# A hybrid decoder step on one core: the front in chunks of 256, 384 and 392 tokens, without index queries for the first

## The chip, the cores and the metric

The kernel is one program on one core of a Trainium2 chip. Its time is device microseconds of one execution, from start to end; less is better. The profile is of one execution of its own, in which the span is the time from the first instruction to the last.

## The reference, cut to what matters

One layer of a hybrid decoder: 1024 prompt tokens (positions 0 to 1023), and 8 sample sequences of one token each behind 1024 cached ones. One input projection feeds sparse attention (group A) and a gated linear recurrence (group B).

```python
h = einsum('btd,de->bte', rms_norm(x, ln_g), w_in)       # D = 1024, columns of 11 parts
# A) lightning indexer, one score for each visible key
s = einsum('bthd,bsd->bths', iq, ik) * IDX_DIM ** -0.5    # 8 index heads of 64
score = einsum('bths,bth->bts', relu(s), iw)
score = where(causal, score, -inf)
_, idx = lax.top_k(score, 256)                            # TOPK_MAX 256, for prompt and sample
out = sparse_attn(q, k[idx], v[idx], ...)                 # 8 heads, 4 kv heads, bias by distance
# B) HGRN2: f = lb + (1 - lb) * sigmoid(h_f); hg = log(f); hk = 1 - f; chunkwise recurrence
S_new, o = gla_chunk(S0, hq, hg, hk, hv)
y = x + concat(a_out * silu(a_gate), rms_norm(h_out) * silu(h_gate)) @ w_out
```

A query at position below 256 sees at most 256 keys, so the top 256 are all of them: its index query decides nothing. Keys, values, index keys and final states are outputs too.

## The kernel before, in words

**Units and jobs.** The input projection is cut into 17 units of 256 columns (`UNITS`; unit 0, the index keys and index weights, has 72). Each unit's weights (1 MB) are loaded by SP into a raw buffer (`load_weights`), rounded by ScalarE to a high half (`high_w`, L1709) and completed by GpSimd to a low half (`split_w`, L555). A job is one output tile: 8 steps of contraction times three products (high x high, low x high, high x low), so 24 matmuls. Jobs of form "T" (units ix, iq and hg; L2321) have the weights stationary and a chunk of tokens moving, `CHUNKS` = 384, 384 and 264 wide; form "N" (L2324) has 128 tokens stationary and 256 columns moving; form "S" (L2313) is the 8 sample tokens of the next unit, from the raw weights. Jobs are numbered in TensorE's order; `JOB0[u]` is the first of group u. Group 0 interleaves ix and iq 0 by chunk (`FRONT`, 9 jobs), then comes iq 1 (6 jobs and an S), gh 0 (8), hg 0, and so on to 128. ScalarE evacuates each job (`evac`), in four banks.

**The front.** For each of three chunks, three row tiles of x are loaded; ScalarE sums their squares (L1674, `squares`), VectorE takes the inverse root (`x_roots`, 11 chained small operations) and scales the rows (L1973; one tile in three by ScalarE), TensorE transposes them in 8 steps (L2176, `transpose_x`), ScalarE writes the high half (L1687) and VectorE the low half (L1981) of each step. The transposes of chunks 1 and 2 are put between the iq jobs of the chunk before (`X_AT`).

**Index scores.** 48 items (tile t = 2 to 7, head h; `ITEMS`) are placed behind the steps of jobs 9 to 20 (`GROUPS`): a product (L2240), ScalarE's relu, VectorE's sum (L2025). GpSimd gathers 32 blocks of cached index keys by indirect DMAs (`load_index_keys`, L1599), each of which waits for the one before, and then cuts the scores causally (L1634).

**The search.** VectorE finds the 256th score of each prompt query by 31 rounds, one bit each (`rounds`: six counts L2060, and L2073 and L2076). The sample's search (L1010 and L1017, `sample_try`, `sample_keep`) has 8 steps between them, after `KEEP_AT` rounds; a step's flags are summed by TensorE behind job `FLAGS_AT` and copied by ScalarE. TensorE waits there for the flags, VectorE at the keep for the copy. The cumulative sums of the recurrence (`scan`, L2084) have fixed places as well: `SCAN_AT` = after rounds 5 and 16, the third behind the last keep. Each scan waits for ScalarE's logarithm (`prep_log`, L1719), which stands behind the second job after its hg unit. After 31 rounds come the masks, and within them VectorE splits the second half of unit 14's weights, which lets SP load the second half of unit 15's (`load_weights` waits for `weights_low_ready`), which job 104 (S) needs.

**The tail.** After job 128 attention runs by head (scores, softmax, transposes, values), with the sample's attention between. Its keys come in 16 groups of four 128 KB pages (`load_key_pages`), the even ones on SP's queue, the odd ones on GpSimd's. GpSimd also loads the recurrence's sample states (1 MB) and spreads the values (two of 512 KB), and updates the states (`sample_state`: L783, L784, L789), with key pages 7, 9 and 11 issued between. The tail ends with the output projection (L1356).

The order on GpSimd at the start of the tail is, before:

```python
load_key_pages(gp, numbers, 3)
gp.dma_start(S0T[...], state...)         # 1 MB
gp.wait_ge(s["hv_out"], 64)
# two broadcasts into VBT, 512 KB each
load_key_pages(gp, numbers, 5)
sample_state()
```

## Time and profile before

| what | value |
|---|---|
| median of three runs | 798.48 us (790.79 to 799.35) |
| the profiled execution, its own time | 795.54 us |
| its span, first to last instruction | 793.5 us |
| mean granted TensorE clock | 0.998 |
| TensorE busy | 755.8 us |
| VectorE busy | 548.4 us |
| ScalarE busy | 420.6 us |
| GpSimd busy | 387.8 us |
| DMA | 83.57 MB, mean 105 GB/s |

The busy time of TensorE counts overlapped ends of matmuls, so it says that there is little idle time, not that every matmul runs at its best. What an engine waited for is shown in brackets in the timeline rows.

### The profile page before, as it was taken

The numbers are of one execution on the slowest core, as the hardware profiler recorded it, in microseconds if no ns is written. First come the engines' busy times: TensorE is split into PE (matmuls) and PEld (weight loads), VectorE is DVE, ScalarE is ACT, GpSimd is POOL, SyncE is SP. The second block draws the span as 40 slices with busy tenths as digits, with TensorE's granted clock in tenths as the row PEclk, the third lists the DMA queues.
The fourth block names the chain that finished last, engine by engine and source line by source line (L and its number), as shares of the span: only waits on it lengthen the run. The fifth ranks groups of instructions, "written<-read, shape, count | busy, mean of one in ns | idle before, by whom it ended". The sixth has DMA issues, their size and how long they took to land.

```text
span 793.5 us, 20224 instructions
## 1 busy us (share of the span) xinstructions
PE 755.8 (95%) x7576; PEld 699.4 (88%) x7576; DVE 548.4 (69%) x1114; ACT 420.6 (53%) x1274; POOL 387.8 (49%) x572
## 2 busy tenths in 40 slices
PE   3999999999999989999999999988999998999998
PEld 3989989899999989999989999966788877898998
DVE  3644767998999989978996946785746368555121
ACT  6765675336465867768465746653535554421210
POOL 3444634437825396648567244239861427510320
PEclk9999999999999999999999999999999999999999
DMA  8303021211102202041203445394584634441632
GB/s 285 93 21 87 14 88 38 74 55 55 55 2 82 91 29 96 29 128 49 93 2 88 140 117 175 103 268 136 142 235 133 204 120 146 135 132 61 230 98 83
DMA packets 69927, 83.57 MB, mean 105 GB/s; under 512 B 20458, under 2 KB 55962, under 8 KB 69578
## 3 DMA queue, kind: packets, MB, share of 16 engines
q1 hardware_dynamic: 65146, 68.68, 27.6%
q0 software_dynamic: 4688, 13.64, 6.1%
q8 instruction: 60, 0.98, 0.5%
q14 instruction: 33, 0.27, 0.1%
HBM read 64.95 MB, written 17.34 MB: 104 GB/s over the span
## 4 chain that ended last, share of the span: by engine, by line
PE 66%; DVE 11%; issue 8%; ACT 6%; POOL 5%; DMA 3%; SPq 0%; DVEq 0%; ACTq 0%; POOLq 0%
PE psum L2324 16%; PE psum L2321 13%; PE psum L1356 11%; PE psum L1289 4%; PE psum L2240 3%; PE psum L1305 3%; DVE flag_count L2060 2%; POOL w_low L555 2%; DMA page_keys<-in_cache_kt 2%; PE psum L1263 1%; PE psum L1269 1%; PE psum L1267 1%; PE psum L2198 1%; DVE bit_kept L2073 1%; PE psum L2176 1%
## 5 line engine op out<-in xcount | busy, mean ns | idle before, releaser
L2324 PE MATMUL psum<-w_high,xT_high 128*128 128x256 f32 x640 | 183.2, 286 | 2.7 <-ACT psum L1832 2.4
L2324 PE MATMUL psum<-w_low,xT_high 128*128 128x256 f32 x640 | 179.5, 280 | 0.0
L2324 PE MATMUL psum<-w_high,xT_low 128*128 128x256 f32 x640 | 179.3, 280 | 0.0
L555 POOL TENSOR_TENSOR w_low<-w_raw,w_high 128x256 fp32r<-128x256 f32 (+1 forms) x144 | 105.2, 768 | 66.2 <-ACT w_high L1709 56.1
L2324 PEld LDWEIGHTS psum<-w_high,xT_high 128*128 128x128 f32 x640 | 120.4, 188 | 5.3 <-ACT psum L1832 3.0
L2324 PEld LDWEIGHTS psum<-w_high,xT_low 128*128 128x128 f32 x640 | 120.4, 188 | 0.4
L2324 PEld LDWEIGHTS psum<-w_low,xT_high 128*128 128x128 f32 x640 | 120.5, 188 | 0.0
L2321 PE MATMUL psum<-xT_high,w_high 128*128 128x384 f32 (+3 forms) x312 | 103.1, 331 | 0.5 <-POOL w_low L555 0.5
L2321 PE MATMUL psum<-xT_low,w_high 128*128 128x384 f32 (+3 forms) x312 | 99.8, 320 | 0.0
L2321 PE MATMUL psum<-xT_high,w_low 128*128 128x384 f32 (+3 forms) x312 | 99.8, 320 | 0.0
L2060 DVE TENSOR_SCALAR_CACHE_REDUCE flag_count<-scores,candidate 128x512 f16<-128x512 f32 (+2 forms) x96 | 96.8, 1008 | 0.0
L2060 DVE TENSOR_SCALAR_CACHE_REDUCE flag<-scores,candidate 128x384 f16<-128x384 f32 (+2 forms) x96 | 84.1, 876 | 9.2 <-DVE candidate L2076 8.6
L927 ACT ACTIVATE prob<-psum,neg_max 128x1024 f32<-128x1024 f32 (+7 forms) x64 | 47.3, 740 | 63.4 <-DVE neg_max L1189 63.2
L1356 PE MATMUL psum<-w_high,xT_high 128*128 128x256 f32 x256 | 73.1, 286 | 0.1
L1356 PE MATMUL psum<-w_low,xT_high 128*128 128x256 f32 x256 | 71.8, 281 | 0.0
L1356 PE MATMUL psum<-w_high,xT_low 128*128 128x256 f32 x256 | 71.7, 280 | 0.0
L1599 POOL DMA_INDIRECT index_keys_T<-in_cache_ikt,index_page_rows x32 | 34.4, 1074 | 55.2 <-DMA index_keys_T<-in_cache_ikt,index_page_rows 53.9
L2321 PEld LDWEIGHTS psum<-xT_high,w_high 128*128 128x128 f32 (+1 forms) x312 | 57.7, 185 | 3.3 <-POOL w_low L555 1.1
L2321 PEld LDWEIGHTS psum<-xT_low,w_high 128*128 128x128 f32 (+1 forms) x312 | 57.7, 185 | 0.8
L2321 PEld LDWEIGHTS psum<-xT_high,w_low 128*128 128x128 f32 (+1 forms) x312 | 57.6, 184 | 0.6
L1189 DVE CUSTOM_DVE_ANT_0 psum<-psum,mask 128x1024 f32<-128x1024 f32 (+5 forms) x48 | 42.9, 898 | 19.9 <-PE psum L1269 19.6
L1827 ACT ACTIVATE stage<-psum 128x256 f32<-128x256 f32 x64 | 24.7, 387 | 56.4 <-PE psum L2324 52.2
(335 smaller groups left out, 1845.3 us busy)
## 6 DMA issues: line engine op xcount, KB each, us to landing
w_raw<-in_w_main SPq DMA_DIRECT2D x40, 512.0 KB, 4.5
x_rows<-in_x_prompt SPq DMA_DIRECT2D x8, 512.0 KB, 6.4
page_keys<-in_cache_kt SPq DMA_DIRECT2D x32, 128.0 KB, 3.8
page_keys<-in_cache_kt POOLq DMA_DIRECT2D x32, 128.0 KB, 3.6
page_values<-in_cache_v SPq DMA_DIRECT2D x32, 128.0 KB, 4.0
page_values<-in_cache_v POOLq DMA_DIRECT2D x32, 128.0 KB, 4.0
x_res<-in_x_prompt SPq DMA_DIRECT2D x32, 128.0 KB
out<-y_rows SPq DMA_DIRECT2D x32, 128.0 KB
```

What stands on the lines that cost most here:

```text
L555: last = gp.tensor_tensor(WL[:, u % 2, 4 * h + k, 0:w], raw(u)[:, h, k, 0:w], f(WH[:, u % 2, 4 * h + k, 0:w]), ALU.subtract)
L927: act.activation(PB[:, m % 3, 0:w], ps(2 * (m % 2), w), ACT.Exp, scale=-1.0, bias=NB[:, h:h + 1], accum_out=RS[:, t % 2, h:h + 1]).then_in ...
L1189: dve.tensor_tensor_reduce(lg, lg, mask, -HD ** -0.5, 3e38, ALU.add, ALU.min, accum_out=NB[:, h:h + 1])\
L1289: last = pe.transpose(ps(4, P, o=b * P), PB[:, m % 3, b * P:(b + 1) * P], IDN[:, :])
L1305: last = pe.matmul(ps(7, P, (g + 1) * HD, g * HD, kv * P), VT[:, b, kv * HD:(kv + 1) * HD], PTS[(2 * p + g) % 3][:, b, :], start=b == 0, s ...
L1356: last = pe.matmul(ps(OBANK[y], UW, rows(i)), a[:, k, row0(i):row0(i) + rows(i)], ww[:, sl, k, :], start=k == 0 and a is XH and ww is WH, ...
L1599: gp.indirect_dma_start(dst, None, cache_ikt.rearrange("a d k -> (a d) k"), bass.IndirectOffsetOnAxis(ap=PGX[:, col:col + 1], axis=0))\
L1827: last = act.activation(STG[0:r, (g + 1) % 4, :], ps(bank, UW, r), fn)
L2060: dve.tensor_scalar((JK, CU)[k % 2][:, 0:w], sc, threshold(k), None, op, ALU.add, accum_out=CNT[:, k:k + 1]).then_inc(s["dve_chain"], 1)
L2240: last = pe.matmul(ps(4 + 2 * (m % 2) + c0 // 512, w), IQS[:, h, (t - 2) * P:(t - 1) * P], stack[:, c0:c0 + w], start=kk == 0, stop=kk == 1)
L2321: last = pe.matmul(ps(BANK[n], cw, m_), ww[:, sl, k, i * P:i * P + m_], x[:, k, t0:t0 + cw], start=first, stop=final)
L2324: last = pe.matmul(ps(BANK[n], w, rows(i)), x[:, k, row0(i):row0(i) + rows(i)], ww[:, sl, k, 0:w], start=first, stop=final)
```

## The change

It does seven things.

1. The chunks of tokens are 256, 384 and 392 wide, not 384, 384 and 264, in every T unit. Their row tiles are (0, 1), (2, 3, 4) and (5, 6, 7, and the 8 sample rows).
2. The index queries of the first chunk (tokens 0 to 255) are not computed: four of the twelve iq jobs go. Group 0 has 7 jobs, iq 1 has 4 and the S; every later job has a number lower by 4.
3. In the front, VectorE scales all rows but tile 7, and sums the squares of tile 3 and of the sample rows; all eight transposes of chunk 1 stand behind job 0, those of chunk 2 in and behind job 3; x's second group is loaded ahead of unit 1's weights, and unit 1's high halves are made apart.
4. The index items stand behind jobs 7 to 16, up to eight in one job.
5. GpSimd's gathers are placed anew around its splits, three of them behind the last causal selects.
6. The sample's index product stands behind jobs 21 and 23 of the new count (25 and 27 of the old), its search begins after 4 rounds, keeps after 6, 8, 10, 12, 15, 17, 23 and 26, flags behind jobs 33, 39, 43, 47, 52, 57, 68, 73; the scans after rounds 5 and 14.
7. On GpSimd, key pages 5 are issued ahead of the state and the spread values.

```diff
-CHUNKS = [(0, 384), (384, 384), (768, 264)]
+CHUNKS = [(0, 256), (256, 384), (640, 392)]
+CHUNK_ROWS = [(0, 1), (2, 3, 4), (5, 6, 7, 8)]
+SQUARES_BY_ACT = [0, 1, 2, 4, 5, 6, 7]
...
-FRONT = [(x, b, c) for c in range(3) for x, b in ((0, 0), (1, 0), (1, 1))]
-IX_JOBS = 7
+FRONT = [(x, b, c) for c in range(3) for x, b in ((0, 0), (1, 0), (1, 1)) if x == 0 or c > 0]
+IX_JOBS = 5
...
-X_AT = {(2, 3): (1, range(4)), (2, 7): (1, range(4, 8)), (4, 7): (2, range(4)), (5, 3): (2, range(4, 8))}
+X_AT = {(0, 7): (1, range(8)), (3, 3): (2, range(4)), (3, 7): (2, range(4, 8))}
...
-        out = [(u, "T", b, c) for c in range(3) for b in range(2)]
+        out = [(u, "T", b, c) for c in (1, 2) for b in range(2)]
...
-GROUPS = {8: [0], 9: [1], 10: [2], 11: [3], 12: [4], 13: [5, 6], 15: [7], 16: [8], 17: [9], 18: [10], 19: [11]}
+GROUPS = {6: [0], 7: [1], 8: [2], 9: [3, 4], 11: [5, 6], 12: [7], 13: [8, 9], 14: [10], 15: [11]}
...
-KEYS_ROWS_AT, SAMPLE_AT, SAMPLE_SUM_AT = 7, 22, 23
-
-FLAGS_AT = {29: 0, 36: 1, 42: 2, 46: 3, 49: 4, 53: 5, 72: 6, 77: 7}
-KEEP_AT = [4, 6, 8, 10, 12, 14, 23, 26]
-SCAN_AT = [5, 16]
+KEYS_ROWS_AT, SAMPLE_AT, SAMPLE_SUM_AT = 5, 21, 23
+
+FLAGS_AT = {33: 0, 39: 1, 43: 2, 47: 3, 52: 4, 57: 5, 68: 6, 73: 7}
+KEEP_AT = [6, 8, 10, 12, 15, 17, 23, 26]
+SCAN_AT = [5, 14]
...
             gp.memset(QPD[:, :, :, :], 0.0).then_inc(s["sample_q_cleared"], 1)
-            load_key_pages(gp, numbers, 3)
+            for n in (3, 5):
+                load_key_pages(gp, numbers, n)
             gp.dma_start(S0T[:, :, :, :], state.rearrange("a k b j v -> (a k) b j v")).then_inc(s["states_in"], 16)
...
-            load_key_pages(gp, numbers, 5)
             sample_state()
...
-            load_weights(sp, 1)
             load_x(1)
-            load_x(2)
...
+            load_weights(sp, 1)
+            load_x(2)
...
-            load_index_keys(0, 0, NPG)
+            load_index_keys(0, 0, 1)
+            split_w(gp, 1)
...
-            load_index_keys(1, 0, 3)
+            load_index_keys(0, 1, NPG)
+            split_w(gp, 2)
             gp.wait_ge(s["x_low_ready"], 3 * KC)
...
-            split_w(gp, 2)
-            load_index_keys(1, 3, NPG)
-            load_index_keys(2, 0, 3)
+            load_index_keys(1, 0, 6)
             split_w(gp, 3)
-            load_index_keys(2, 3, NPG)
-            load_index_keys(3, 0, NPG)
+            load_index_keys(1, 6, NPG)
+            load_index_keys(2, 0, NPG)
+            load_index_keys(3, 0, 5)
...
                     for t in range(2, NT):
+                        if t == NT - 1:
+                            load_index_keys(3, 5, 6)
                         gp.wait_ge(s["index_scores_added"], 24 + 4 * (t - 1))
...
                     split_w(gp, u + 1)
+                    load_index_keys(3, 6, NPG)
...
             x_roots(0)
             for i in (0, 1):
                 scale_rows(i)
+            square(3)
             dve.wait_ge(s["gain_in"], 16)
             low_x(0, range(KC))
             x_roots(1)
-            for i in (3, 4):
+            for i in CHUNK_ROWS[1]:
                 scale_rows(i)
...
-            rounds(0, 2)
+            rounds(0, 4)
             sample_scores()
...
-                pe.wait_ge(s["x_rows_scaled"], 2 * c + 2)
-                pe.wait_ge(s["x_rows_scaled_act"], c + 1)
+                pe.wait_ge(s["x_rows_scaled"], (2, 5, 8)[c])
+                if c == 2:
+                    pe.wait_ge(s["x_rows_scaled_act"], 1)
```

## Rows read from the trace of the kernel before

**Rows 1.** The page: shares of the chain that ended last

```profile
PE 66%; DVE 11%; issue 8%; ACT 6%; POOL 5%; DMA 3%; SPq 0%; DVEq 0%; ACTq 0%; POOLq 0%
```

**Rows 2.** The chain in order of time: start us, us, engine, tile, line, count

```profile
34.22 8.38 PE psum L2321 x48
...
347.16 34.28 PE psum L2324 x288
```

**Rows 3.** Timeline, first 20 us: start us, us, engine, line, operation [idle before <-releaser]

```profile
7.85 1.06 ACT L1674 ACTIVATE square_junk<-x_rows 128x1024 bf16<-128x1024 f32 x1 [0.88 <-DMA x_rows<-in_x_prompt]
...
11.31 1.41 DVE L1973 TENSOR_SCALAR x_rows<-x_rows,x_stats 128x1024 f32<-128x1024 f32 x2
...
12.82 5.35 PE L2176 MATMUL psum<-ident,x_rows 128*128 128x128 f32 x24 [12.82 <-DVE x_rows L1973]
...
18.03 1.99 ACT L1687 ACTIVATE xT_high<-psum,ln_gain 128x384 fp32r<-128x384 f32 x4
...
18.63 2.19 DVE L1981 SCALAR_TENSOR_TENSOR xT_low<-psum,ln_gain,xT_high 128x384 fp32r<-128x384 f32 x4 [1.74 <-ACT xT_high L1687]
```

**Rows 4.** Timeline of GpSimd: one index gather; the last causal select

```profile
41.73 0.94 POOL L1599 DMA_INDIRECT index_keys_T<-in_cache_ikt,index_page_rows  x1 [1.74 <-DMA index_keys_T<-in_cache_ikt,index_page_rows]
...
137.26 0.29 POOL L1634 TENSOR_SCALAR_AFFINE_SELECT scores<-scores 128x128 f32<-128x128 f32 x1 [2.93 <-DVE scores L2025]
```

**Rows 5.** Timeline of VectorE, the search from 244 to 424 us

```profile
244.40 0.15 DVE L1017 TENSOR_SCALAR bit_kept<-enough_sum 128x1 int32<-128x1 f32 x1 [0.20 <-DVE candidate L2076]
...
259.71 0.15 DVE L1017 TENSOR_SCALAR bit_kept<-enough_sum 128x1 int32<-128x1 f32 x1 [0.20 <-DVE candidate L2076]
...
274.48 2.29 DVE L2084 TENSOR_TENSOR_SCAN decay_log<-scan_keep,decay_log 128x1024 f32<-128x1024 bf16 x1 [0.20 <-DVE candidate L2076]
...
283.24 0.61 DVE L2060 TENSOR_SCALAR_CACHE_REDUCE flag<-scores,candidate 128x384 f16<-128x384 f32 x1 [0.42 <-DVE candidate L2076]
...
289.92 0.61 DVE L2060 TENSOR_SCALAR_CACHE_REDUCE flag<-scores,candidate 128x384 f16<-128x384 f32 x1 [0.41 <-DVE candidate L2076]
...
302.21 4.59 DVE L2073 SCALAR_TENSOR_TENSOR bit_kept<-count,bit_value 128x6 int32<-128x6 f32 x1
...
352.48 2.29 DVE L2084 TENSOR_TENSOR_SCAN decay_log<-scan_keep,decay_log 128x1024 f32<-128x1024 bf16 x1 [2.83 <-ACT decay_log L1719]
...
423.67 0.43 DVE L555 TENSOR_TENSOR w_low<-w_raw,w_high 128x256 fp32r<-128x256 f32 x1 [1.38 <-POOL w_low L564]
```

**Rows 6.** The page: groups of instructions, count, busy us, mean ns, idle before

```profile
L555 POOL TENSOR_TENSOR w_low<-w_raw,w_high 128x256 fp32r<-128x256 f32 (+1 forms) x144 | 105.2, 768 | 66.2 <-ACT w_high L1709 56.1
```

**Rows 7.** Timeline of ScalarE around the second decay logarithm

```profile
266.33 1.25 ACT L1719 ACTIVATE decay_log<-decay_log,lb,one_minus_lb 128x1024 f32<-128x1024 f32 x1
```

**Rows 8.** The chain in order of time, around 425 us

```profile
425.12 5.91 DMA w_raw<-in_w_main
```

**Rows 9.** Timeline of TensorE: two starts after idle time

```profile
292.11 0.39 PE L2324 MATMUL psum<-w_high,xT_high 128*128 128x256 f32 x1 [1.27 <-ACT psum L1832]
...
431.29 0.91 PE L2313 MATMUL psum<-w_raw,x_sample_T 128*8 128x64 f32 x52 [0.53 <-DMA w_raw<-in_w_main]
```

**Rows 10.** Timeline of GpSimd from 523 us: key pages 5, first state product

```profile
523.65 2.91 POOL L624 DMA_DIRECT2D page_keys<-in_cache_kt  x4
...
536.65 0.61 POOL L783 TENSOR_TENSOR state_in<-state_in,f_sample 128x256 f32<-128x256 f32 x1 [10.10 <-DMA v_spread<-hv_spill]
```

**Rows 11.** Timeline of TensorE: key page products one and two

```profile
522.20 1.07 PE L1383 MATMUL psum<-page_keys,q_padded 128*32 128x256 f32 x16
...
538.18 1.93 PE L1383 MATMUL psum<-page_keys,q_padded 128*32 128x256 f32 x16 [4.82 <-DMA page_keys<-in_cache_kt]
```

**Rows 12.** DMA by queue in 524 to 530 us: packets, MB, share of 16 engines

```profile
q0 software_dynamic: 244, 1.60, 87.7%
...
q1 hardware_dynamic: 447, 0.22, 15.5%
```

**Rows 13.** Windows: stretch, length, busy (count) by engine, TensorE clock, DMA share, GB/s

```profile
536.00:540.00 4.00, 1.82 (x16) 0.59 (x16) 0.00 (x0) 0.00 (x0) 3.35 (x6) 0.71 0.89 226
```

More of the change, by code:

```diff
@@ L124 @@
     JOB0.append(JOB0[-1] + len(jobs(_u)))
-LOWS = JOB0[2] + 6
+LOWS = JOB0[2] + 4
 ORDERED = [job for _u in range(NU) for job in jobs(_u)]
@@ L1461, in load_x @@
             def load_x(g):
-                for i in range(3 * g, 3 * g + 3):
+                for i in CHUNK_ROWS[g]:
                     sp.dma_start(x_buf(i)[0:rows(i)], x_rows(i)).then_inc(s[f"x_in{i}"], 16)
@@ L1688, in high_x, with high_half @@
                         .then_inc(s["x_high_ready"], 1)
+            def high_half(u, h):
+                w = width(u)
+                if u == 1:
+                    act.wait_ge(s[f"second_weights_in{h}"], 16)
+                else:
+                    act.wait_ge(s[f"weights_in{h}"], 16 * max(u, 1))
+                act.activation(WH[:, u % 2, 4 * h:4 * h + 4, 0:w], raw(u)[:, h, :, 0:w], ACT.Copy)\
+                    .then_inc(s["weights_high_ready"], 1)
             def high_w(u):
-                w = width(u)
                 if u == 2:
@@ L1704, in high_w @@
                 for h in range(2):
-                    if u == 1:
-                        act.wait_ge(s[f"second_weights_in{h}"], 16)
-                    else:
-                        act.wait_ge(s[f"weights_in{h}"], 16 * max(u, 1))
-                    act.activation(WH[:, u % 2, 4 * h:4 * h + 4, 0:w], raw(u)[:, h, :, 0:w], ACT.Copy)\
-                        .then_inc(s["weights_high_ready"], 1)
+                    high_half(u, h)
             def prep_log(j):
@@ L1866, in _ @@
             act.activation(RS[:, 0, 0:1], CNT[:, 0:1], ACT.Square)
-            for i in range(3):
+            for i in (0, 1):
                 squares(i)
             high_w(0)
-            scale_rows(2)
+            squares(2)
             act.wait_ge(s["gain_in"], 16)
-            high_x(0, range(4))
-            high_w(1)
-            high_x(0, range(4, KC))
-            for i in range(3, 6):
-                squares(i)
+            high_x(0, range(KC))
+            squares(4)
+            high_half(1, 0)
             for u in (0, *range(2, NU)):
@@ L1884, in _ @@
                     if n == 1:
-                        for i in (6, 7):
+                        for i in (5, 6, 7):
                             squares(i)
-                        scale_rows(5)
-                    if n == 2:
-                        squares(NT)
+                    if n == IX_JOBS - 1:
+                        high_w(2)
                     if (n, 3) in X_AT:
@@ L1895, in _ @@
                     evac(u, q)
-                    if n == 3:
+                    if n == 1:
                         scale_rows(7)
-                    if (n, 7) in X_AT:
+                    if n == 0:
+                        high_x(1, range(4))
+                        high_half(1, 1)
+                        high_x(1, range(4, KC))
+                    elif (n, 7) in X_AT:
                         high_x(*X_AT[n, 7])
@@ L1954, in _, with square @@
             dve.wait_ge(s["init_dve"], 1)
+            def square(i):
+                r = rows(i)
+                dve.wait_ge(s[f"x_in{i}"], 16)
+                link(dve.tensor_tensor_reduce(CU[0:r, 0:D].bitcast(BF16), x_buf(i)[0:r], x_buf(i)[0:r], 1.0, 0.0, ALU.mult, ALU.add,
+                                              accum_out=STAT[0:r, 0, i:i + 1]))
             def x_roots(g):
-                c = slice(3 * g, 3 * g + 3)
-                dve.wait_ge(s["x_squares_ready"], 3 * g + 3)
+                c = slice(CHUNK_ROWS[g][0], CHUNK_ROWS[g][-1] + 1)
+                dve.wait_ge(s["x_squares_ready"], sum(i <= CHUNK_ROWS[g][-1] for i in SQUARES_BY_ACT))
                 x, y, tmp = STAT[:, 1, c], STAT[:, 3, c], STAT[:, 2, c]
@@ L2111, in _ @@
                         low_x(*X_AT[n, 3])
+                    if n == 1:
+                        square(NT)
+                        x_roots(2)
+                        for x in (5, 6, NT):
+                            scale_rows(x)
                     if n < LOWS:
@@ L2116, in _ @@
                     if n == 2:
-                        x_roots(2)
-                        for x in (6, NT):
-                            scale_rows(x)
-                    if n == 4:
                         constants()
@@ L2131, in _ @@
             sample_try(dve, link, 0)
-            done = 2
+            done = 4
             for r in range(SROUNDS):
@@ L2168, in transpose_x @@
                     pe.wait_ge(s["ident_in"], 16)
-                pe.wait_ge(s["x_rows_scaled"], 2 * c + 2)
-                pe.wait_ge(s["x_rows_scaled_act"], c + 1)
+                pe.wait_ge(s["x_rows_scaled"], (2, 5, 8)[c])
+                if c == 2:
+                    pe.wait_ge(s["x_rows_scaled_act"], 1)
                 for k in ks:
-                    if c > 0 or k == 7:
-                        pe.wait_ge(s["x_low_ready"], KC * c + k - 3 if c > 0 else 1)
-                    for i in range(3 * c, 3 * c + 3):
+                    same = [j for j in range(k) if x_bank(c, j) == x_bank(c, k)]
+                    if c > 0 or same:
+                        pe.wait_ge(s["x_low_ready"], KC * c + (same[-1] + 1 if same else 0))
+                    for i in CHUNK_ROWS[c]:
                         r = rows(i)
@@ L2307, in unit @@
                             pe.wait_ge(s["x_low_ready"], KC * c + k + 1)
+                        if u == 1 and k == 4:
+                            pe.wait_ge(s["weights_low_ready"], 2 * u + 2)
                         if k % 2 == 1:
```

19 lines of the change are left out of this document (8 added, 11 removed).

## The prediction

> **What bounds the kernel now.** I read the page first: TensorE is busy for 755.8 us (the table above), and the chain of work that ended last runs 66% over it and 11% over VectorE [rows 1]. The chain in order of time then says where it leaves TensorE: hardly ever up to the last causal select at 137.26 [rows 4]; from hg 0 on it goes through VectorE's search and comes back to TensorE by the cumulative sums. So there are two long threads side by side, and the reader is to see how tightly they are tied. TensorE stood 1.27 us at 292.11 behind the second scan, and 0.53 us at 431.29 for raw weights [rows 9]. Those weights were released by VectorE, which split its half at 423.67 after waiting 1.38 us for GpSimd [rows 5]; the load took 5.91 us more [rows 8]. VectorE, then, has 1.4 us in hand there and TensorE none. The third place is the start of the tail: TensorE stood 4.82 us at 538.18 for key pages [rows 11].
>
> **The work that goes.** A 384 wide matmul comes every 8.38 / 48 = 0.1746 us, a 256 wide one every 34.28 / 288 = 0.1190 us [rows 2], so a column costs 0.434 ns. Four iq jobs of 384 go: 4 x 24 x 0.1746 = 16.8 us. The other side is that the third chunk is wider by 128 columns, in the four iq jobs that have it: 4 x 24 x 128 x 0.434 ns = 5.3 us. In ix and hg the first chunk gives what the third takes, and the transposes are as many as before. Net 11.4 us of TensorE, nearly all of which lies on the path up to 137 us.
>
> **The front.** The roots of the first group now want two squares, not three; the third had waited 0.88 us and taken 1.1 [rows 3], so the roots start 2.0 us earlier and the first transpose at 10.8 us instead of 12.82. Eight steps of 256 columns, at two thirds of the 0.50 us on ScalarE (1.99 / 4) and 0.55 on VectorE (2.19 / 4) plus fixed parts [rows 3], and the square that VectorE now does before them (an operation it has not in the trace; over 1024 elements a tile its scaling takes 0.71 us [rows 3] and its scan 2.29 [rows 5]; I take 1.2), put the end of job 0 at about 16.2. TensorE then stands, for nothing lies between: ScalarE's fourth square ends at 16.1, the root's 11 small steps take 2.3 us (from 8.9, the third square's end, to 11.31 [rows 3]), three scalings of 0.71 us (1.41 for two [rows 3]) 2.1, so the transposes of chunk 1 start at 20.5 and the ix job behind them ends at 27.4, paced by ScalarE (8 x 0.50, and 1.0 of high weights between) and VectorE. Before, that point was reached at 34.22 + 24 x 0.1746 = 38.4 [rows 2]. So the front is 11.0 us ahead there. From there to the last item: two jobs of 384 less (8.4), five jobs 128 columns wider (6.7 more), one more row tile transposed in chunk 2 (0.9 more), and waits of about 1.7 us, since VectorE's constants stand ahead of the low halves of chunk 2; together 10.1 to 10.8 ahead. I take **10.5**. Two covers could be gone. GpSimd gathers every 2.7 us (0.94 and 1.74 of waiting [rows 4]); seven of them now stand ahead of unit 2's split, which I put at 53 us, 3 us before TensorE wants it at 56. The 29th is done at about 126 us, as the last scores come; before, GpSimd stood 2.93 us for them at 137.26 [rows 4], so this margin is used up and a slip would show at hg 0, whose split ends about when TensorE gets there (132 us): 0 to 3 us, taken at 0. Eight items in one job are 0 to 2 us of waiting for the relu, 1 of which is in the 10.5.
>
> **The search.** It starts 10.5 us earlier. The 14th round ended at 259.71; with one sample step fewer (15.3 us for two rounds with a step, from 244.40 to 259.71, less twice the 6.68 from 283.24 to 289.92, is 1.9; less twice the 6.4 at other places, 2.5: I take 2.3 [rows 5]) VectorE now comes to the second scan at 259.7 - 10.5 - 2.3 = 246.9, or 250 if flags that sit behind later jobs make it wait. But the scan wants ScalarE's logarithm, which ends at 266.33 + 1.25 = 267.6 before [rows 7] and stands behind TensorE's hg 1: 257.1 now. **VectorE stands there 7 to 10 us**, and what it saved is lost. From the scan's end (276.8 before [rows 5], 259.4 now) to its split it took 422.3 - 276.8 = 145.5 us with 15 rounds. Now 17 rounds and two more sample steps are left: two rounds with a step are the 15.3, the other step 2.3, and the third scan's wait of 2.83 [rows 5] goes. VectorE is at its split at 259.4 + 145.5 + 15.3 + 2.3 - 2.8 = 419.7, 2.6 us earlier than before. The split takes 1.45, the load 5.91 [rows 8], and TensorE starts the sample job at 427.2 instead of 431.29, **4.1 us** earlier. It would be there at 420.3; it loses the 6 to 7 us at this job, or before it: at the summing of sample flag 5, and behind the third scan, whose sums come only 2.7 us earlier. The 1.27 us behind the second scan [rows 9] goes, but is inside this bound. What follows to the end of the projection hangs on this job (the fourth logarithm, unit 15's split), so 4.1 us are carried on.
>
> **The tail.** GpSimd issued the state and the values just ahead of key pages 5 at 523.65; its first state product waited for them until 536.65 [rows 10]. In 524 to 530 us its queue (q0) had 87.7% of the DMA engines' time for 1.60 MB, and SP's (q1) 15.5% for 0.22 MB [rows 12]; both at once wanted to move pages of 128 KB. TensorE's second product waited for the pages of both queues that had been asked for before the state. With the state 2.9 us later (the time of the four issues at 523.65 [rows 10]) pages 2 and 3 have the engines to themselves and should land by 530, ahead of need. The 4.82 us go, and so does the cold start: in 536 to 540 the granted clock was 0.71 of full speed, and the product took 1.93 us where its like took 1.07 [rows 11, 13]: 0.9 us. What is late next: GpSimd's state products, which start when the spread values land and have pages 7, 9, 11 and 13 queued among and behind them. TensorE wants page 7 some 5.7 us sooner while the products start 0 to 3 us later. That gives back 0 to 5.7 us; as the first of these pages is wanted only some heads later, I take the lower part, 1.7 back and **4.0** kept.
>
> **The sum.** The profiled execution took 795.5 us: 795.5 - 4.1 - 4.0 = 787.4. It lies 2.9 us under the median of the three runs, which spread from 790.8 to 799.4, so I forecast 788. A difference of 1% (8 us) is about what a measurement of this kernel can tell from none.
>
> **The rivals.** *The relief is carried whole.* If VectorE isn't held at the second scan, or has fewer of the long stalls below, TensorE keeps its 10.5 us: 795.5 - 10.5 - 5 = 780. For it: the scans, flags and keeps are laid out as if no such wait were there (flag 5 is summed behind a job which TensorE reaches at 265, before VectorE has it ready by my count). Against it: logarithm and round counts are fixed by the code. It decides if VectorE reaches its split by 413. *The gap in the tail stays*, because SP's pages wait behind the values that it loads itself, or the state's delay costs as much: 795.5 - 4.1 = 791.4. *Slower.* In the 31 rounds three L2073 took long; the one at 302.21 took 4.59 us for 6 elements [rows 5], while GpSimd split weights. The moved rounds meet the splits anew. Three further such stalls behind the second scan, 13.8 us, fall on the thread that has no slack: 795.5 - 4.1 + 13.8 = 805. It decides once the new ones sum to over 4.1 us more than the old.
>
> The Trainium skill (SBUF — State Buffer, Who interferes with whom) says that such a VectorE instruction and a GpSimd one block each other for the length of one instruction. One split instruction is 768 ns on average [rows 6], so by the rule the stall at 302.21 would be under 0.8 us, not 4.59; the row shows several in a line. By the rule the thread would be 3.8 us shorter after the second scan both before and now, and the last rival would have no price.
>
> **How the numbers follow.** The forecast's case has 0.38 (784 to 792), the whole relief 0.27 (776 to 784), the gap that stays 0.16 (790 to 794), slower 0.12 (799 to 812), the rest 0.07. The range is 777 to 799. Faster by over 1% (under 790.5): the whole relief and most of the forecast's case, 0.57; within 1%: 0.35; slower by over 1%: the upper half of the last rival and some of the rest, 0.08.
>
> **What would show it.** In the changed trace: no idle on TensorE between first chunk and second would refute the front; idle there of some 4 us and hg 0 beginning at about 132 us would bear it out. The wait of the second scan for ScalarE's L1719, 7 us or more, with the sample job of unit 15 waiting for its raw weights by several us, is the step that the forecast hangs on. In the tail, the second key product should start without a wait and at full clock, and a wait at the fourth or seventh says what was given back. The prediction is wrong if VectorE's rounds behind the scan are faster than these, if GpSimd's gathers come after the scores, or if TensorE's idle time in the front brings down its clock for longer than it stood cold at the start.

## The result, and the profile after

The changed kernel takes 790.65 us, the median of 20 runs (785.03 to 795.05), where the kernel before, run beside it, takes 796.53 (790.79 to 800.14, 20 runs). The ratio is 0.992, with a 95% interval of 0.9903 to 0.9936. The forecast was 788. The profiled execution took 791.76 us with a span of 790.1, 3.8 and 3.4 us less than before's; it lies 1.1 us above the changed kernel's median, before's 1.0 below its own.

The page of the changed kernel, shares of the chain that ended last (to be held against [rows 1]):

```profile
PE 56%; DVE 18%; issue 13%; ACT 5%; POOL 5%; DMA 3%; SPq 1%; DVEq 0%; POOLq 0%; ACTq 0%
```

VectorE's share has grown from 11 to 18%: TensorE is tied to the search more tightly than before. The timeline of TensorE, changed kernel (start, us, engine, line; in brackets the idle time before and its releaser), against [rows 3, 9, 11]:

```profile
11.11 3.52 PE L2195 MATMUL psum<-ident,x_rows 128*128 128x128 f32 x16 [11.11 <-DVE x_rows L1988]
...
20.61 3.79 PE L2195 MATMUL psum<-ident,x_rows 128*128 128x128 f32 x19 [3.01 <-DVE x_rows L1988]
...
168.44 1.08 PE L2334 MATMUL psum<-w_raw,x_sample_T 128*8 128x64 f32 x64
...
270.69 0.16 PE L2299 MATMUL psum<-enough,same_row 128*128 128x1 bf16 x1 [3.55 <-DVE enough L1014]
...
421.70 0.39 PE L2345 MATMUL psum<-w_high,xT_high 128*128 128x256 f32 x1 [1.80 <-DVE w_low L557]
425.96 1.08 PE L2334 MATMUL psum<-w_raw,x_sample_T 128*8 128x64 f32 x64 [1.15 <-DMA w_raw<-in_w_main]
...
517.56 1.07 PE L1385 MATMUL psum<-page_keys,q_padded 128*32 128x256 f32 x16
528.67 1.07 PE L1385 MATMUL psum<-page_keys,q_padded 128*32 128x256 f32 x16
...
547.38 1.94 PE L1385 MATMUL psum<-page_keys,q_padded 128*32 128x256 f32 x16 [4.48 <-DMA page_keys<-in_cache_kt]
```

Read downwards, it is an account of the lead over before. TensorE starts 1.7 us earlier (11.11). At the sample products within the jobs of hv 0 (168.44, before 176.78) it leads by 8.3. At 270.69 it stands 3.55 us for sample flag 5. At unit 15's sample job it is 5.3 ahead (425.96, before 431.29), at the first key product 4.6 (517.56, before 522.20). The second key product has no wait any more, but the fourth has one of 4.48, and the end is 3.4 us ahead. VectorE's timeline, changed kernel, against [rows 5]:

```profile
199.35 5.76 DVE L2088 SCALAR_TENSOR_TENSOR bit_kept<-count,bit_value 128x6 int32<-128x6 f32 x1
...
259.40 2.29 DVE L2099 TENSOR_TENSOR_SCAN decay_log<-scan_keep,decay_log 128x1024 f32<-128x1024 bf16 x1 [9.31 <-ACT decay_log L1728]
...
292.37 1.84 DVE L2088 SCALAR_TENSOR_TENSOR bit_kept<-count,bit_value 128x6 int32<-128x6 f32 x1
...
378.46 3.77 DVE L2088 SCALAR_TENSOR_TENSOR bit_kept<-count,bit_value 128x6 int32<-128x6 f32 x1
...
420.21 1.43 DVE L557 TENSOR_TENSOR w_low<-w_raw,w_high 128x256 fp32r<-128x256 f32 x4
```

The second scan waits 9.31 us for ScalarE's logarithm. The long L2088 (before, L2073) are three as before, and two are shorter: 5.76 where 7.35 stood, 1.84 where 4.59 stood. VectorE is at its split at 420.21. GpSimd in the tail, changed kernel, against [rows 10]:

```profile
521.45 0.56 POOL L828 DMA_DIRECT2D state_in<-in_state  x1
...
535.77 0.62 POOL L785 TENSOR_TENSOR state_in<-state_in,f_sample 128x256 f32<-128x256 f32 x1 [12.69 <-DMA v_spread<-hv_spill]
...
542.38 2.94 POOL L626 DMA_DIRECT2D page_keys<-in_cache_kt  x4
```

GpSimd waits 12.69 us for the spread values, and only behind eight state products asks for pages 7, at 542.38; TensorE wants them at 547.38 - 4.48 = 542.9. Three stretches where the clock was low, changed kernel, by windows (stretch, length, busy time and count of each engine, TensorE's clock, DMA share, GB/s):

```profile
20.00:24.00 4.00, 3.39 (x19) 3.40 (x20) 3.56 (x7) 3.46 (x8) 3.17 (x5) 0.65 0.94 296
24.00:28.00 4.00, 4.00 (x25) 3.45 (x24) 3.20 (x6) 3.91 (x8) 3.07 (x5) 0.92 0.62 177
```
```profile
270.00:274.00 4.00, 3.31 (x17) 3.34 (x18) 3.91 (x12) 3.08 (x12) 0.41 (x3) 0.57 0.09 33
```
```profile
547.00:551.00 4.00, 3.62 (x26) 2.39 (x27) 0.14 (x1) 0.60 (x1) 3.92 (x8) 0.59 0.02 6
```

Each follows an idle time of TensorE (3.01, 3.55 and 4.48 us). Before, the clock was 1.00 in 20 to 28 us.

### The profile page after: what moved, and what is told of

The parts are those of the page before. It is cut to its first block, busy times and chain, and to the rows that moved or that the text cites. A ratio compares the mean times of both kernels' runs of the same rounds, so it can differ in the third digit from the quotient of the medians.

```text
span 790.1 us, 20005 instructions
## 1 busy us (share of the span) xinstructions
PE 746.7 (95%) x7480; PEld 689.7 (87%) x7480; DVE 555.1 (70%) x1112; ACT 415.2 (53%) x1260; POOL 389.7 (49%) x572
## 4 chain that ended last, share of the span: by engine, by line
PE 56%; DVE 18%; issue 13%; ACT 5%; POOL 5%; DMA 3%; SPq 1%; DVEq 0%; POOLq 0%; ACTq 0%
PE psum L2345 13%; PE psum L1358 11%; PE psum L2342 10%; DVE flag_count L2075 4%; PE psum L1291 3%; PE psum L2259 3%; PE psum L1307 3%; POOL w_low L557 3%; DVE flag L2075 2%; DVE bit_kept L2088 1%; PE psum L2195 1%; PE psum L1269 1%; PE psum L1265 1%; PE psum L1271 1%; DVE flag_count L973 1%
## 5 line engine op out<-in xcount | busy, mean ns | idle before, releaser
L557 POOL TENSOR_TENSOR w_low<-w_raw,w_high 128x256 fp32r<-128x256 f32 (+1 forms) x144 | 107.7, 784 | 61.7 <-ACT w_high L1702 50.4
L2342 PE MATMUL psum<-xT_high,w_high 128*128 128x392 f32 (+5 forms) x280 | 93.5, 334 | 0.0
L2342 PE MATMUL psum<-xT_low,w_high 128*128 128x392 f32 (+5 forms) x280 | 90.7, 324 | 0.0
L2342 PE MATMUL psum<-xT_high,w_low 128*128 128x392 f32 (+5 forms) x280 | 90.6, 324 | 0.0
L1601 POOL DMA_INDIRECT index_keys_T<-in_cache_ikt,index_page_rows x32 | 36.7, 1146 | 51.9 <-DMA index_keys_T<-in_cache_ikt,index_page_rows 50.1
L1702 ACT ACTIVATE w_high<-w_raw 128x1024 fp32r<-128x1024 f32 (+1 forms) x42 | 41.5, 1027 | 28.1 <-DMA w_raw<-in_w_main 19.3
L2342 PEld LDWEIGHTS psum<-xT_high,w_high 128*128 128x128 f32 (+1 forms) x280 | 51.5, 184 | 2.4 <-POOL w_low L557 0.2
L2342 PEld LDWEIGHTS psum<-xT_low,w_high 128*128 128x128 f32 (+1 forms) x280 | 51.5, 184 | 0.7
```

What stands on the lines that cost most here:

```text
L557: last = gp.tensor_tensor(WL[:, u % 2, 4 * h + k, 0:w], raw(u)[:, h, k, 0:w], f(WH[:, u % 2, 4 * h + k, 0:w]), ALU.subtract)
L1601: gp.indirect_dma_start(dst, None, cache_ikt.rearrange("a d k -> (a d) k"), bass.IndirectOffsetOnAxis(ap=PGX[:, col:col + 1], axis=0))\
L1702: act.activation(WH[:, u % 2, 4 * h:4 * h + 4, 0:w], raw(u)[:, h, :, 0:w], ACT.Copy)\
L2342: last = pe.matmul(ps(BANK[n], cw, m_), ww[:, sl, k, i * P:i * P + m_], x[:, k, t0:t0 + cw], start=first, stop=final)
```

## The experiments

Each kernel was run beside the kernel before; ratios are to that one, with 95% intervals. Those of 1, 2, 3 and 5 were run together, those of 4, 6 and the first of 7 as well, and the last two of 7 with 8 and 9. A profile is of one execution, and the fronts differ from one to the next; where that bears on a comparison, it is said.

**1. The second scan behind round 16.**

```
-SCAN_AT = [5, 14]
+SCAN_AT = [5, 16]
```

> The changed kernel with one number altered: the second scan stands behind round 16 of the search again, not behind round 14. In the changed kernel VectorE stood 9.31 us before that scan for ScalarE's logarithm, and TensorE 3.55 us at 270.69 for sample flag 5. Theory (the scan is placed ahead of its logarithm and holds both threads): VectorE comes to the scan at about 263.5 and waits under 1 us; flag 5 is ready some 9 us earlier, so TensorE's 3.55 us go; VectorE reaches its split at 412 to 415 instead of 421.70, the sample job starts at 418 to 421 instead of 425.96, and the whole is 5 us shorter, 784 to 787, ratio to the kernel before 0.985. Rival A (another thing holds the thread next: the third logarithm, longer L2088, GpSimd's split): the sample job starts within 2 us of 425.96, the time is 789 to 791. Rival B (the tail, not the search, sets the end): the sample job is 5 to 7 us earlier and the end moves by under 2 us.

784.65 us (784.24 to 785.39, 4 runs), ratio 0.9848 (0.9793 to 0.9902). VectorE's and TensorE's timelines of this kernel:

```profile
261.79 2.29 DVE L2099 TENSOR_TENSOR_SCAN decay_log<-scan_keep,decay_log 128x1024 f32<-128x1024 bf16 x1 [0.21 <-DVE candidate L2091]
```
```profile
416.55 1.08 PE L2334 MATMUL psum<-w_raw,x_sample_T 128*8 128x64 f32 x64 [0.18 <-issue]
...
527.38 1.07 PE L1385 MATMUL psum<-page_keys,q_padded 128*32 128x256 f32 x16 [1.59 <-DMA page_keys<-in_cache_kt]
...
539.48 1.94 PE L1385 MATMUL psum<-page_keys,q_padded 128*32 128x256 f32 x16 [5.03 <-DMA page_keys<-in_cache_kt]
```

The theory holds, and the interval lies just clear of the changed kernel's (0.9903 to 0.9936): neither the scan nor flag 5 waits, and TensorE no longer stands at the sample job. That job comes 9.4 us before that of the changed kernel, of which 3.0 were already there at the sample products of hv 0's jobs (165.40), where the edit can't reach, so the search gave 6.4. Some of it is lost in the tail, where the waits are now 1.59 and 5.03.

**2. The flag alone.** `FLAGS_AT`: flag 5 behind job 60, not 57.

> The changed kernel with sample flag 5 summed behind job 60, not behind job 57; the second scan stays behind round 14. Theory (VectorE's thread, which waits 9.31 us at the scan, sets the sample job): TensorE's 3.55 us at 270.69 go but come back later, the sample job of unit 15 starts within 1 us of 425.96, the time is 790 to 791.5. Rival (the place of the flag on TensorE is what costs): the sample job and the end are 3 us earlier, 787 to 788.

791.46 us (787.99 to 801.63, 10 runs), 0.9921 (0.9888 to 0.9955): nothing gained, as the theory has it. The scan still waited 9.32 us. In the profile the 3.55 us are gone from flag 5, but the sample job is not within 1 us of 425.96; it is late, at 428.75, for another reason (VectorE, then TensorE at flag 7):

```profile
281.52 8.05 DVE L2088 SCALAR_TENSOR_TENSOR bit_kept<-count,bit_value 128x6 int32<-128x6 f32 x1
```
```profile
333.85 0.16 PE L2299 MATMUL psum<-enough,same_row 128*128 128x1 bf16 x1 [7.63 <-DVE enough L1014]
```

An instruction on 6 elements took 8.05 us here; the one behind the second scan took 1.84 in the profile of the changed kernel.

**3 and 4. The tail's order, undone in the changed kernel (3, the edit shown) and alone in the kernel before (4, the reverse edit).**

```
-            for n in (3, 5):
-                load_key_pages(gp, numbers, n)
+            load_key_pages(gp, numbers, 3)
             gp.dma_start(S0T ...
...
+            load_key_pages(gp, numbers, 5)
             sample_state()
```

> The changed kernel with the tail's order put back: GpSimd issues the state and the spread values ahead of key pages 5. Front and search are as changed. Theory (the tail edit only moves the gap from the second key product to the fourth): the second product waits 4 to 5 us and the fourth not at all, GpSimd's first state product starts 2 to 3 us earlier, and the time is within 1.5 us of the changed kernel's 790.65: 790 to 792, ratio to before 0.992 to 0.995. Rival (my prediction's 4.0 us for the tail hold): 794 to 795, ratio 0.998.

> The kernel before with the tail's new order alone (GpSimd issues pages 3 and 5, then the state and the spread values). Theory (the gap moves from the second key product to the fourth, and is somewhat smaller): the second product without a wait, the fourth with 4 to 5 us; 793 to 796 where the kernel before has 797.2, ratio 0.996 to 1.0. Rival (my prediction's 4.0 us hold): 792.5 to 793.2, ratio 0.995, and no wait over 1 us before the fourth.

Undone: 792.96 us (786.44 to 799.35, 10 runs), 0.9937 (0.9902 to 0.9972), between the theory's 790 to 792 and the rival's 794 to 795. Alone: 796.62 us (793.08 to 799.16, 10 runs), 1.000 (0.9979 to 1.0021). TensorE undone, then alone:

```profile
533.90 1.94 PE L1385 MATMUL psum<-page_keys,q_padded 128*32 128x256 f32 x16 [7.27 <-DMA page_keys<-in_cache_kt]
```
```profile
552.33 1.94 PE L1383 MATMUL psum<-page_keys,q_padded 128*32 128x256 f32 x16 [4.76 <-DMA page_keys<-in_cache_kt]
```

In the kernel before, the new order only moves the gap, 4.82 us at the second product [rows 11] to 4.76 at the fourth; from the first key product to the end of the span it took 271.3 us without the edit and 271.4 with it. Behind the new front it is worth something: TensorE is there earlier and would have waited 7.27, and the same stretch took 276.1 us undone and 272.5 in the changed kernel. The profiles say 3.6 us, the medians 2.3 with overlapping intervals, so its size isn't settled.

**5. Pages 7 ahead of the wait.**

```
             def sample_state():
+                load_key_pages(gp, numbers, 7)
                 gp.wait_ge(s["states_in"], 48)
...
-                    if b == 3:
-                        load_key_pages(gp, numbers, 7)
```

> The changed kernel with one GpSimd load moved: key pages 7 are issued behind the spread values' issue and ahead of the wait for them, not behind the eighth state product. Theory (pages 7 come late only because GpSimd's queue holds them behind products that wait 12.69 us for the spread values): they are issued by 525 instead of 542.38 and land by 541; the fourth key product starts at 542.9 without its 4.48 us and at full clock (0.9 more), and the time is 4 to 5 us shorter, 785.5 to 787, ratio 0.987. Rival (what is late next are the values and the pages behind them, or the wait for page 9 takes its place at the fifth product): 789 to 791. Rival (pages 7 delay the spread values on the same queue by 3 us and with them the state, pages 9 to 15 and the values): 791 to 794.

786.97 us (785.06 to 791.92, 4 runs), 0.9866 (0.981 to 0.9922), within the theory's range, though the interval still overlaps the changed kernel's, so the gain is read from the trace. The profiled run was the slowest, 791.92, and shows both sides. The fourth product, at 548.14, waits for nothing, and from the first product to the end of the span it took 267.3 us, 5.2 less than in the changed kernel. Ahead of that, this run had lost as much in the search (TensorE; VectorE; GpSimd):

```profile
426.50 0.58 PE L2344 MATMUL psum<-w_high,xT_high 128*128 128x256 f32 x1 [6.63 <-DVE w_low L557]
```
```profile
371.24 11.00 DVE L2087 SCALAR_TENSOR_TENSOR bit_kept<-count,bit_value 128x6 int32<-128x6 f32 x1
```
```profile
372.48 2.82 POOL L1573 TENSOR_TENSOR q_decayed<-q_decayed,hq 128x256 f32<-128x256 f32 x4
375.25 5.58 POOL L557 TENSOR_TENSOR w_low<-w_raw,w_high 128x256 fp32r<-128x256 f32 x8
380.77 1.45 POOL L1583 TENSOR_TENSOR intra<-intra,intra_mask 128x256 f32<-128x256 f32 x2
```

VectorE's instruction begins while GpSimd is in a row of 24 instructions without a break and ends at 382.24; GpSimd's row ends at 382.22. It is so each time: 213.44 and 213.42 in the kernel before (the L2073 of 7.35 us at 206.09), 289.57 and 289.54 in experiment 2. VectorE's counts (L2074, one tensor operand) aren't held: over 1024 columns one took 1.28 us at 369.82, within the row, and another 1.28 at 387.10, where GpSimd did little.

**6. GpSimd's rows with breaks.** In hg stages 0 to 2 GpSimd waits for each product of the decayed keys and intra queries and each weight split to end before the next:

```
                 last = gp.tensor_tensor(QI[:, t], QI[:, t], QB[:, t], ALU.mult)
+                if x < 3:
+                    link(last)
```

and so in `decayed_keys` and `split_half`.

> The changed kernel, in which GpSimd waits for each of its multiplications of the decayed keys and the intra queries and of its four weight splits behind them to end before it issues the next, in hg stages 0 to 2 (nothing is left out). Theory (VectorE's L2088 can't begin until GpSimd's unbroken row of instructions ends; in the changed kernel 5.76 us from 199.35, the row ending at 205.08; in another run 11.00 us from 371.24, the row ending at 382.22): with a break behind each, no L2088 takes over 1.5 us; VectorE has 5.6 us less behind the second scan, less what GpSimd's later work costs; the sample job of unit 15 starts 3 to 5 us earlier than 425.96 and the time is 786 to 788, with runs closer to each other than the 785 to 795 of the changed kernel. Rival A (one block lasts one instruction, as the skill's page on SBUF has it, and the long L2088 have another cause): they stay at 4 to 8 us and the time at 790 to 792. Rival B (the breaks lengthen GpSimd's work by over 3 us a stage, and hg's sums come later): over 791.

787.91 us (784.57 to 789.47, 4 runs), 0.9879 (0.984 to 0.9917), an interval that overlaps the changed kernel's. None of the 31 (L2094 in this kernel) takes over 0.77 us, so their length was set by the unbroken row. The Trainium skill (SBUF — State Buffer, Who interferes with whom) says that a VectorE instruction with two inputs in SBUF contends with a GpSimd instruction that reads it, and that the block lasts for one instruction. With breaks the trace agrees (one split took 0.73 us); without them it lasted some 15 of GpSimd's in experiment 5. The sample job came at 424.14, 1.8 us earlier than in the changed kernel, not 3 to 5, and 1.0 of that was there at hv 0 already (167.44). What was saved ahead of the scan was lost there, as its wait grew to 10.29. What was saved behind it, TensorE could not use: it stood 3.55 us at flag 5, which comes behind the scan, ran at 0.50 of its clock in 270 to 274, and came to the split and the sample job without a wait. So by this trace the time at flag 5, which is hidden in the changed kernel, begins to count once VectorE is faster. The breaks cost as well: the eight splits behind 199.94 took 6.32 us, not 5.58.

> The changed kernel with all three edits: scan behind round 16, pages 7 early, GpSimd's rows broken up. Theory: with the scan behind round 16 TensorE had no wait at the sample job (0.18 us), so VectorE is off the path there, and its shorter rounds are worth nothing more: within 1.5 us of the kernel with the first two edits, 779 to 781. Rival (VectorE's thread still sets part of it): 2 to 4 us less, 776 to 778.

782.53 us (782.46 to 782.59, 4 runs), 0.9824 (0.9797 to 0.985): outside the theory's 779 to 781, and by the median 1.9 us slower than the same kernel without breaks (780.66, next experiment), with intervals that overlap. Its trace has one wait of TensorE that the other's lacks, at hg 1:

```profile
298.73 0.45 PE L2246 MATMUL psum<-hv,intra 128*64 128x64 f32 x8 [1.62 <-POOL intra L1589]
```

But its four runs lie within 0.13 us, where the changed kernel's twenty spread over 10.

**7. Both single edits, and the front's idle time filled.**

> The changed kernel with both single edits: the second scan behind round 16, and pages 7 issued ahead of the wait for the spread values. Theory (two separate costs, one on the way to the sample job, one in the tail): they add up. With the scan alone the tail had waits of 1.59 and 5.03 us before the third and fourth key products; the second of them and its half-clock product (0.9) go: 784.65 less 5 to 6, 779 to 781, ratio to the kernel before 0.978. Rival (the tail is bound by what its queues can bring, so that an earlier start buys only longer waits there): 783 to 785.

780.66 us (778.36 to 785.1, 4 runs), 0.9812 (0.9766 to 0.9858). The costs add up (6.0 and 3.7 us by the medians alone, 10.0 together); the fourth product has no wait. The interval overlaps that of experiment 1, so what pages 7 add is again the trace's to say. Then 24 products that nobody reads, between job 0 and chunk 1:

```
+                    if n == 0:
+                        for k in range(KC):
+                            for x, ww in ((XH, WH), (XL, WH), (XH, WL)):
+                                pe.matmul(ps(x_bank(1, 0), 256, XW), ww[:, 0, k, 0:XW], x[:, k, 0:256], start=True, stop=True)
```

> The changed kernel, in which TensorE fills its idle time between job 0 and the transposes of chunk 1 with 24 products that nobody reads (matmuls of job 0 once more, 72 by 256, into the bank that the first of these transposes overwrites: 24 x 0.119 = 2.9 us). In the changed kernel it stood 3.01 us before 20.61, and the granted clock in 20 to 24 us was 0.65; in the kernel with the scan behind round 16 it stood 2.67 us and the clock stayed 1.00, and unit 2's sample job came at 85.52 instead of 88.59. Theory (the idle time brings the clock down and costs 2 to 3 us more than itself): the clock stays 1.00 in 20 to 28, unit 2's sample job comes at 85.0 to 86.0; VectorE is held by its scan, of which the logarithm comes earlier by as much, so the end gains 2 to 3 us in the profiled run, 787 to 789. Rival (the low clock of that stretch has another cause, or chunk 1's transposes are paced by ScalarE and VectorE anyway): the sample job at 88 to 89, the time at 790 to 791.

790.9 us (788.83 to 794.27, 10 runs), 0.9925 (0.9902 to 0.9949): no gain, as the rival has it. Windows, then VectorE, then TensorE of this kernel:

```profile
20.00:24.00 4.00, 2.70 (x25) 2.46 (x23) 3.48 (x7) 1.69 (x5) 2.95 (x3) 1.00 1.02 297
```
```profile
129.27 0.55 DVE L2075 TENSOR_SCALAR_CACHE_REDUCE flag<-scores 128x384 f16<-128x384 f32 x1 [1.85 <-POOL scores L1638]
```
```profile
134.82 0.38 PE L2342 MATMUL psum<-xT_high,w_high 128*128 128x256 f32 x1 [1.00 <-POOL w_low L557]
```

The clock stays 1.00. But the transposes of chunk 1 start at 21.73, 1.1 us later than in the changed kernel, for their rows came later, and the ix job ends at 28.69, only 0.4 earlier. Unit 2's sample products come at 86.79, 1.8 us earlier and short of the theory's 85.0 to 86.0; the other 1.4 us are at the index items, where this profile lacks two waits for the relu (0.40 and 0.43 at 77.64 and 81.07 in the changed kernel's). Even that doesn't arrive. VectorE waits 1.85 us for GpSimd's last causal selects, and TensorE 1.00 for hg 0's split; the search starts at 129.27, 0.3 earlier than in the changed kernel (129.56), and the scan waits its 9.31 us. The late selects are this profile's: with the same filling, in the next kernel and in 9, GpSimd waited 2.50 and 2.59 us for the scores, so what held the median of ten runs isn't shown. With experiment 7's two edits as well:

> The changed kernel with the second scan behind round 16, pages 7 issued early, and the 24 unread products in the front's idle time. Theory: the kernel with the first two took 780.66, with 0.58 of the clock in 20 to 24 us in its profile; with the clock at 1.00 it is 2 to 3 us shorter, 777.5 to 779. Rival (none of the front's gain arrives): 780 to 781.

781.48 us (778.47 to 782.32, 4 runs), 0.9816 (0.9763 to 0.987): just above the rival's 780 to 781, no gain that shows.

**8. The search's old plan on the new front.** Flags, keeps and first try as before, moved by four jobs; the second scan behind round 16.

> The changed kernel with the search's plan as it was, moved by the four jobs that are gone: first sample try behind round 2, flags behind jobs 25, 32, 38, 42, 45, 49, keeps behind rounds 4, 6, 8, 10, 12, 14, second scan behind round 16. Front and tail as changed. Theory (of the re-placement only the scan's place matters): as the kernel with the scan behind round 16, 784.65: 783.5 to 786.5, and no wait over 2 us at the scan or at a flag. Rival (the new places of flags and keeps are worth something, since TensorE with the old ones waits for flags that VectorE, which comes 8 us earlier together with it, has not ready): waits of 1 to 4 us at the flags and 788 to 791.

792.66 us (789.38 to 797.23, 10 runs), 0.9943 (0.991 to 0.9975). My theory fell: it is 8 us slower than experiment 1, which differs from it in flags, keeps and first try alone, and no run of the one is as fast as the slowest of the other (789.38 and 785.39). VectorE, then TensorE:

```profile
153.91 1.23 DVE L2058 COPY scores_sample<-psum 128x1025 f32<-128x1025 f32 x1 [5.15 <-PE psum L2293]
...
202.80 8.74 DVE L2088 SCALAR_TENSOR_TENSOR bit_kept<-count,bit_value 128x6 int32<-128x6 f32 x1
```
```profile
214.48 0.16 PE L2299 MATMUL psum<-enough,same_row 128*128 128x1 bf16 x1 [2.64 <-DVE enough L1014]
...
286.03 0.56 PE L2345 MATMUL psum<-w_high,xT_high 128*128 128x256 f32 x1 [3.09 <-ACT psum L1841]
```

After two rounds VectorE stands 5.15 us for the sample's scores, which TensorE makes at a fixed job; with four rounds first, as changed, that wait is gone. Its stall at the next GpSimd row is 8.74 us, where experiment 1's was 5.75, and it comes to its second scan at 272.77, 11.0 us after experiment 1. Of these, 5.15 are the wait, 3.0 the longer stall, and 2.8 no doing of the edit: this profile's search started that much later (129.29 and 126.52), behind a front with a low clock (0.67 in 24 to 28 us). TensorE waits behind flag and scan. The rival had the waits at the flags (2.64 at one) but not the larger one at the scores.

**9. All of it, breaks in every second place.**

> As the last, and GpSimd waits for its own instruction to end in every second place of its rows (at most four in a row, 2.8 us, where breaks behind each cost TensorE 1.62 us at a masked intra product and VectorE 1.79 at its split). Theory (breaks don't speed up the likeliest run, as VectorE is off the path there; they take away the long L2088 of 8 to 11 us that some runs have): no L2088 over 3 us, 777.5 to 780, runs within 1 us of each other where those of the kernel without breaks spread over several us. Rival (the breaks still cost GpSimd more than they save): 781 to 782.

779.55 us (777.76 to 780.62, 4 runs), 0.9793 (0.9739 to 0.9847), the fastest of all by the median and 11 us below the changed kernel. It isn't told apart from the 780.66 and 781.48 of the kernels without breaks. The longest L2088 is 0.75 us, as expected. Its runs spread over 2.9 us, not 1.

## Why the prediction was right, and where it was off

**The work that goes.** 11.4 us of TensorE were forecast. Its busy time fell from 755.8 to 746.7, 9.1; the two stretches at a low clock in 20 to 28 us can hold up to 1.7 of the rest (4 x 0.35 + 4 x 0.08).

**The front.** First transpose 10.8 forecast, 11.11 measured; chunk 1's transposes 20.5 and 20.61; TensorE stood 3.01 us. But the end of the ix job was put at 27.4 and came at 29.1, and the lead at the last item was 8.0 us, not 10.5. Of the missing 2.5 us, about 1.5 are the clock behind the idle time, which I named as a danger and priced at nothing. The profile of experiment 5 shows it best: TensorE stood as long there, 2.99 us, kept 1.00 in 20 to 28, and needed 7.0 us from the first transpose of chunk 1 (20.89) to the end of the ix job (27.86), where the changed kernel needed 8.5 (20.61 to 29.13).

```profile
20.89 2.95 PE L2194 MATMUL psum<-ident,x_rows 128*128 128x128 f32 x24 [2.99 <-DVE x_rows L1987]
```
```profile
20.00:24.00 4.00, 3.11 (x26) 2.95 (x27) 3.49 (x7) 2.67 (x6) 2.81 (x4) 1.00 0.99 292
```

The rest arises behind it. In experiment 1, also at 1.00, the lead at hv 0 was 11.4 (165.40 against 176.78); in experiments 2, 3 and 5, at 1.00 as well, 9.4 to 9.9. Between the two lie the waits for the relu near 76 to 81 us, which some profiles have and others not; why, no run shows. (The written-out terms for the ix job, 8 x 0.50 and 1.0, make 5.0 of the 6.9 us between 20.5 and 27.4; the sum was right at full clock all the same.) GpSimd's margin I called used up and priced at 0 with 0 to 3 as its bounds. The price is right, the reason isn't: GpSimd still stood 4.24 us for the last scores, before 2.93. In experiment 7's profile with the gap filled it had none.

**The search.** VectorE came to the scan at 250.1, the later of the two times that I gave, and the wait, forecast at 7 to 10 us, was 9.31; that it decides is shown by experiments 1 and 2. The sample job was forecast 4.1 us earlier and was 5.3, and that it came so near owes something to luck. The front's lead was 2.5 less, so the logarithm ended at 259.4, not 257.1; the L2088 behind the scan was 1.84 us, not 4.59; the two nearly cancel, and VectorE was at its split at 420.21 for the 419.7 forecast. The gain over the forecast is the weights' load, which I had taken over at 5.91 us. In the chain of the changed kernel:

```profile
421.67 4.05 DMA w_raw<-in_w_main
```

The 3.55 us at flag 5 stood where I had put them. They, and the clock of 0.57 behind them, cost nothing in this kernel, as TensorE waits for the split and the load later (1.80 and 1.15 us).

**The tail.** The step that failed is "as the first of these pages is wanted only some heads later, I take the lower part, 1.7 back and 4.0 kept". Pages 7 are wanted at the fourth product, 14 us behind the second, and GpSimd asks for them half a microsecond before. 4.48 us of waiting and a half-clock product came back, near the upper of the bounds 0 to 5.7, and the stretch as a whole lies beyond it: from the first key product to the end of the span it took 1.2 us more than before, where 4.0 less were forecast. By the waits and products at the page keys alone it would have come out about even; where the other 1.5 us went isn't shown. Experiment 4 has it by itself, 1.000.

**The sum.** In the profiled pair TensorE led by 4.6 at the first key product, less 1.2, 3.4 in all, against 8.1 forecast; the medians differ by 5.9. The time, 790.65, lies near the upper end of the likeliest case's range of 784 to 792. It stays inside because that range is wide: its second term, the tail's 4.0, was not there. Of the chances, the largest went to a kernel faster by over 1% (0.57); the measured 0.992, with its whole interval, is within 1% (0.35).

**The rivals.** *The gap in the tail stays*, 791.4 with a range of 790 to 794 and a chance of 0.16, also holds the measured time, and for its second reason, that the state's delay costs as much, the traces speak: experiment 4's 1.000, and 791.76 us for the profiled execution. So the time doesn't choose between the forecast's case and this rival; the tail's mechanism is the rival's, but for the 2.3 to 3.6 us that experiment 3 gives the new order behind the new front. The whole relief was to decide by VectorE reaching its split by 413; it was there at 420.21. With the scan moved it was there at 410.61 (experiment 1), and with pages 7 as well the time is this rival's 780 (780.66, first of experiment 7). The slower rival has a real mechanism, and one that changes from run to run: stalls of 8.05 and 11.00 us stood in the profiles of experiments 2 and 5 where the changed kernel's had 1.84 and 3.77. By the rule of one instruction it would have had no price; the rows show that the stall lasts longer. It didn't decide the median.

## What to carry to other kernels

When an early stage gets shorter, list for each later wait the event that doesn't move with it: a scan placed by round count, the sample's scores made at a fixed job, pages asked for behind a wait. The scan's place cost 6 us (790.65 to 784.65), the search's old plan would have cost 8 more (experiment 8 against 1), and with the scan and the pages moved the kernel took 780.66. An edit of a load order that closes one gap should be followed to the next page on the same queue before its gain is booked.

## What the chip showed that I had not expected

- A VectorE instruction with two tensor operands, on 6 elements, took up to 11.00 us: until the end of GpSimd's unbroken row (382.24 and 382.22). Over 31 rounds these instructions came to 29.0 us in that run, and to 9.4 in the kernel with a break behind each GpSimd instruction (group lines of the profiles of experiment 5 and of the breaks with both edits). The next instruction of each round, also with two tensor operands, grows instead, from 10.7 us in all to 14.0:

```profile
L2087 DVE SCALAR_TENSOR_TENSOR bit_kept<-count,bit_value 128x6 int32<-128x6 f32 x31 | 29.0, 935 | 3.8
```
```profile
L2093 DVE SCALAR_TENSOR_TENSOR bit_kept<-count,bit_value 128x6 int32<-128x6 f32 x31 | 9.4, 304 | 3.7
```

- Some of what looks like noise may be this meeting: the changed kernel's runs spread over 10 us, those with all breaks over 0.13. But experiment 1, without breaks, spread over only 1.2, and these are four runs each, so how much of the spread it makes stays open.
- How long TensorE stood in the front doesn't alone say whether its clock falls: behind 3.01 us (changed kernel) it was 0.65 in 20 to 24, behind 2.92 (first of experiment 7) 0.58, but behind 2.99 (experiment 5) 1.00, as behind 2.67 and 2.24 (experiments 1 and 2). Filled, as in the rest of experiment 7, it stayed 1.00.
